# Neighbourhood attention in a fused two-block transformer: two PSUM banks each for scores and transposed probabilities, and the next item's transposition ahead of this item's values

## What is computed

```python
def neighbourhood_attention(q, k, v, rpb):
    ...
        sc = jnp.einsum('bchd,brcwhd->bhcrw', qr, kn) * scale + bias[None]
        sc = sc.reshape(bn, h, GRID_W, wh * ww).astype(jnp.float32)
        pr = jax.nn.softmax(sc, axis=-1).astype(v.dtype).reshape(bn, h, GRID_W, wh, ww)
        return jnp.einsum('bhcrw,brcwhd->bchd', pr, vn)
...
    h = h + (g_attn * y_attn + g_ssm * y_ssm) @ w_out[i]
```

## Time and profile before

| | |
|---|---|
| median of 3 runs | 3952.51 us (3952.14 to 3955.69) |
| the profiled execution | 3956.39 us |
| its span, first to last instruction | 3954.5 us |
| busy: PE, DVE, ACT, POOL | 91%, 61%, 28%, 51% of the span |
| mean granted TensorE clock | 0.951 of full speed |
| neighbourhood attention, `scores(0)` to the end of the last values | 3294.8 to 3433.8 us |
| its steady part, `scores(3)` on | from 3314.2 us |

### The profile page before, as it was taken

The page is one execution under the profiler, slowest core; times in us unless marked ns, Lnnn a source line. Parts: engine busy times, 40 slices in busy tenths (PEclk is TensorE's granted clock), DMA queues, the critical chain, the costliest instruction groups (busy, mean ns, idle before and its releaser), DMA issues.

```text
span 3954.5 us, 50521 instructions
## 1 busy us (share of the span) xinstructions
PE 3591.8 (91%) x20020; PEld 3070.1 (78%) x20020; DVE 2412.0 (61%) x3010; ACT 1094.4 (28%) x1848; POOL 2025.6 (51%) x1100
## 2 busy tenths in 40 slices
PE   8899788999999989788899999999957777999997
PEld 7798678899999779666778888888846664578886
DVE  7786798774333867688967333333278884563335
ACT  4406432222210422633132220121033334322201
POOL 4254235466666535433656666666633442356664
PEclk9799899999999979999999999999978888999999
DMA  3122111222223212111222223222311122222232
GB/s 133 44 89 73 33 44 64 64 87 89 90 91 101 97 48 86 59 38 43 80 69 93 93 96 101 96 95 96 106 55 59 62 77 88 73 87 94 95 109 72
DMA packets 91424, 313.29 MB, mean 79 GB/s; under 512 B 10240, under 2 KB 12544, under 8 KB 91264
## 3 DMA queue, kind: packets, MB, share of 16 engines
q1 hardware_dynamic: 80064, 289.44, 22.2%
q10 hardware_dynamic: 11200, 21.71, 1.5%
HBM read 304.82 MB, written 6.29 MB: 79 GB/s over the span
## 4 chain that ended last, share of the span: by engine, by line
PE 65%; DVE 23%; ACT 9%; issue 3%; POOL 0%; DMA 0%; ACTq 0%; DVEq 0%; POOLq 0%
PE acc L446 19%; PE acc L447 18%; PE acc L449 18%; DVE cu L1725 7%; DVE trs L1596 2%; PE aux L592 1%; DVE rh L1683 1%; PE aux L660 1%; PE aux L739 1%; DVE w L1884 1%; PE aux L675 1%; DVE zz L2006 1%; PE acc L689 1%; ACT yv L1349 1%; DVE rb L1680 1%
## 5 line engine op out<-in xcount | busy, mean ns | idle before, releaser
L419 POOL TENSOR_SCALAR whi<-raw 128x1024 fp32r<-128x1024 f32 x548 | 615.5, 1123 | 1855.0 <-PE acc L449 1834.0
L421 POOL TENSOR_TENSOR wlo<-raw,whi 128x1024 fp32r<-128x1024 f32 x548 | 1410.3, 2573 | 45.7
L446 PE MATMUL acc<-nhi,whi 128*128 128x512 f32 (+1 forms) x2776 | 956.7, 353 | 56.6 <-DVE mt L1734 25.7
L447 PE MATMUL acc<-nlo,whi 128*128 128x512 f32 (+1 forms) x2776 | 950.3, 351 | 0.0
L449 PE MATMUL acc<-nhi,wlo 128*128 128x512 f32 (+1 forms) x2776 | 871.3, 349 | 0.0
L446 PEld LDWEIGHTS acc<-nhi,whi 128*128 128x128 f32 x2776 | 528.7, 190 | 142.3 <-issue 53.4
L447 PEld LDWEIGHTS acc<-nlo,whi 128*128 128x128 f32 x2776 | 528.0, 190 | 68.3
L446 PE MATMUL acc<-bhi,whi 128*128 128x264 f32 (+1 forms) x1864 | 560.7, 317 | 17.9 <-ACT rg L1075 11.8
L447 PE MATMUL acc<-blo,whi 128*128 128x264 f32 (+1 forms) x1864 | 545.2, 309 | 0.0
L449 PEld LDWEIGHTS acc<-nhi,wlo 128*128 128x128 f32 x2776 | 489.2, 191 | 68.8
L1725 DVE SCALAR_TENSOR_TENSOR cu<-cx,par,cu 128x528 f32<-128x528 f32 (+1 forms) x480 | 489.6, 1074 | 0.0
(11 more groups left out here) (359 smaller groups left out, 4764.8 us busy)
## 6 DMA issues: line engine op xcount, KB each, us to landing
raw<-in_w SPq DMA_DIRECT2D x548, 512.0 KB, 3.3
merge_gates<-gout ACTq DMA_DIRECT2D x16, 256.0 KB, 2.8
natab<-in_natab ACTq DMA_DIRECT2D x4, 896.0 KB, 7.4
h<-in_h ACTq DMA_DIRECT2D x8, 264.0 KB, 6.6
rope<-in_rope ACTq DMA_DIRECT2D x2, 1056.0 KB, 7.1
rnn_w<-in_gate ACTq DMA_DIRECT2D x2, 1024.0 KB, 10.0
sbc<-in_ssm ACTq DMA_DIRECT2D x4, 512.0 KB, 3.5
sg<-merge_gates ACTq DMA_DIRECT2D x8, 256.0 KB, 3.5
```

The lines of the kernel that those rows point to most:

```text
L419: pool.tensor_scalar(hi, w, 1.0, 0.0, ALU.mult, ALU.add).then_inc(sem("w_hi"), 1)
L421: pool.tensor_tensor(lo, w, hi.bitcast(F32), ALU.subtract).then_inc(sem("w_split"), 1)
L446: pe.matmul(acc[s][:, f, 0:TH], hi, xh[:, f * TH:(f + 1) * TH], start=a, stop=False)
L447: pe.matmul(acc[s][:, f, 0:TH], hi, xl[:, f * TH:(f + 1) * TH], start=False, stop=False)
```

## The change

`scores(j)` writes bank `j % 2` of `aux[0]` and `turn(j)` bank `j % 2` of `aux[1]`; the readers on VectorE and ScalarE follow. `scores(j)` waits for the score step of item j - 2 and not j - 1, and `turn(j)` for the copy of j - 2 and not j - 1. `turn(j + 1)` stands between `merge_part(j)` and `values(j)`; it stood behind `values(j)`. The work itself, `pts2` and the lists of VectorE and ScalarE stay as they are.

```diff
@@ tensor engine, neighbours()
                 def scores(j):
...
-                    if j:
-                        pe.wait_ge(sem("na_scored"), j)
-                    pe.matmul(aux[0][:, 0, :], q2[rows, hh // 2, i * P:(i + 1) * P], k2[rows, hh // 2, :],
+                    if j >= 2:
+                        pe.wait_ge(sem("na_scored"), j - 1)
+                    pe.matmul(aux[0][:, j % 2, :], q2[rows, hh // 2, i * P:(i + 1) * P], k2[rows, hh // 2, :],
                               start=True, stop=True).then_inc(sem("na_s"), 1)
 
                 def turn(j):
                     pe.wait_ge(sem("na_p"), j + 1)
-                    if j:
-                        pe.wait_ge(sem("na_pt"), j)
+                    if j >= 2:
+                        pe.wait_ge(sem("na_pt"), j - 1)
                     for c in range(4):
-                        m = pe.transpose(aux[1][:, 0, c * P:(c + 1) * P], sm2[:, j % 3, c * P:(c + 1) * P], ident[:, :])
+                        m = pe.transpose(aux[1][:, j % 2, c * P:(c + 1) * P], sm2[:, j % 3, c * P:(c + 1) * P], ident[:, :])
...
                 scores(0)
                 scores(1)
+                turn(0)
                 for j in range(len(items)):
-                    turn(j)
                     if j + 2 < len(items):
                         scores(j + 2)
                     merge_part(j)
+                    if j + 1 < len(items):
+                        turn(j + 1)
                     values(j)
@@ scalar engine
-                    act.activation(pts2[:, :, :], aux[1][:, 0, :].rearrange("p (a b) -> p a b", a=4), ACT.Copy)\
+                    act.activation(pts2[:, :, :], aux[1][:, j % 2, :].rearrange("p (a b) -> p a b", a=4), ACT.Copy)\
@@ vector engine
-                    dve.tensor_tensor_reduce(sm2[:, b], aux[0][:, 0, :], add, 1.0, CHOSEN, ALU.add, ALU.max,
+                    dve.tensor_tensor_reduce(sm2[:, b], aux[0][:, j % 2, :], add, 1.0, CHOSEN, ALU.add, ALU.max,
```

## The result

| | before | changed |
|---|---|---|
| median of 4 runs | 3952.32 us (3950.69 to 3955.69) | 4003.82 us (3998.71 to 4009.52) |
| the profiled execution's span | 3954.5 us | 4007.6 us |
| granted clock, mean | 0.951 | 0.941 |

The ratio is 1.0128, with a 95% interval from 1.0113 to 1.0143: 51 us more. Forecast were 3992 us and a range up to 4004. The direction was right, and so was the loop between the two engines that makes the first half of the loss. The term for the low clock was less than half of what it measured, and the time is 12 us over the forecast. That it still lies in the range, by 0.2 us, is luck.

The account below looks back on a forecast made before the run. TensorE was taken to bound undisturbed items (3.55 us), VectorE's chain the borders of heads. Loop 26.2, start 1.1, end 0.8 and low clock 11 sum to +39.1 us: median about 3992 us, range 3977 to 4004.

Parts of the forecast that it names:

- The loop: Scores, VectorE's scaling, earlier transposition, values set the item period: 4.38 us undisturbed, 138.1 us for 28 periods, +26.2 us.
- Banks and copy: Second banks remove only the second scores product's wait; the copy into single pts2 stays hidden, 2.6 us to spare.
- Start and end: Stage's start up to scores(3) costs +1.1 us; its end, from scores(31) to the last values, +0.8 us.
- The neighbours: New instruction pairs on TensorE, values before scores and transposition before values: 0.1 us an item either way, taken as 0.
- The clock term: TensorE's new gaps in the stage bring some 26 us at the low clock level, costing 11 us.
- the clock falls and stays down longer: Rival for the stage: 45 us at the low level, all on the path, +50 us, 4003 us; chance 0.12.
- the clock holds: Rival: the stage's clock stays at 1.00 despite the longer gaps, +28 us, 3981 us; chance 0.22.
- What the profile was to show: In the stage: about 29 transposition waits for the scaling, 37 us; items of 4.4, 5.4 or 6.0 us; PEclk about 0.9.
- The rival of the faster side: Scaling is done before the earlier transposition, all the stage's waits go, 13.6 us gained, 3939 us; chance 0.04.

## Why the prediction came out as it did

**The loop was right, term by term.** Scores to transposition 2.69 us (2.70 forecast), undisturbed period 4.30 (4.38), with the product 5.36 (5.43), 28 periods at the full clock 136.4 (138.1, by the run with three unread matmuls), so +24.5 us where +26.2 was forecast. The 0.08 us is in the transposition, which the values follow 0.59 us behind its start and not 0.66: the 2.70 us ran from the scores' start in the timeline, which is 0.07 us ahead of their start in the chain, while 0.66 and 1.02 were lengths in the chain, so 0.07 us were counted twice.

**Banks and copy were right.** Nothing for the banks, and no matmul waits for the copy into the single `pts2`.

**Start and end were right.** From `scores(0)` (3295.47) to `scores(3)` 20.7 us where it was 19.4: +1.3, and +1.1 was forecast. The values of the last item end 3486.44 + 1.02 - 3478.88 = 8.6 us behind `scores(31)` (8.5 forecast).

**The neighbours were right in the bounds and wrong in the value.** In the changed kernel they are hidden by the wait, so 0 was right there. Out of the wait, they gain 0.15 us an item, a little more than the 0.1 allowed.

**The clock term failed.** Forecast were 26 us at the low level and 11 us of time, measured 78 us and 26.3 us. The step at fault is the scaling by the first block's attention: equal idle time was to bring equal low time, in stretches as short as the one of 3.3 us in the earlier trace rows. The price of a low microsecond, 11 / 26 = 0.42 forecast and 26.3 / 78 = 0.34 measured, was not at fault.

The number of falls was about right: in the trace of before the 27 us at 0.50 of the first block's attention are eight stretches of 3.4 us each, and here there are seven. Their length was not: four of the seven last 7 to 31 us, through items that follow one another with no gap (the row from 3361.2 to 3376.5 above). So a gap could cost whole items of 6.60 us, not one stretch.

The rival "the clock falls and stays down longer", which had 0.12, is what happened; it was priced at 4003 us from 45 us at the low level, all on the path, where there are 78, partly on it. That 4003 is so near the measured 4003.82 is therefore luck as well, and the range reached to 4004 only because half of this rival was taken in.

The Trainium skill (TensorE: Matmul & The Clock Gate, a second failure mode) tells of a kernel that cycles through PSUM banks, idles briefly and often between groups of matmuls, and has its clock swing by it. The trace agrees on the short idling, with 0.76, though not on the banks: the kernel with the banks alone lost nothing, and the order alone, with one bank each, had 0.72.

**One reading for the rival "the clock holds" was wrong.** It says that the stage stood at 1.00 through waits up to 1.6 us. That wait, 1.57 us ahead of 3307.06, is at the start, where the clock was low: the transposition behind it took 1.12 us. In the part at 1.00 no wait for the scaling was over 0.8 us, so that rival had less for it than its 0.22.

**What the profile was to show.** Forecast were 29 waits and 37 us for the scaling and a clock of about 0.9; the stage behind its start has 24 waits, 31 us and 0.76. The waits are fewer because in the items without a gap, all at 0.50, the scaling is done before TensorE gets to the transposition.

**The rival of the faster side** named the right point of decision, when the scaling ends, and took VectorE's list as a given. It was that list that could move: there the waits do go. The 3939.56 us are near the 3939 of that rival, but not by its sum: the gain was 15.6 us where it had 13.6, and 4.2 of it are the neighbours, which it had at nothing.

**Left open.** Why the low level outlasts its gap at some borders of this stage, with TensorE busy all the time, and not at others or in the first block's attention, was not settled. Filling the gaps shows that they bring it on, not what ends it.

## What to carry to other kernels

When an instruction is moved ahead on one engine, look up what stands in front of its input in the other engine's list. An engine that is early only waits, and all that was moved behind the wait joins the loop; here the cure was to move the producer too, and that alone had most of the gain. And where a change opens gaps on TensorE, price the low clock as a cost of its own, with a wide range: here it was as dear as the loop itself, and a few unread matmuls took it away.

## What the runs showed of the hardware

- At 0.50 an item without a gap takes 6.60 us where 4.30 with a gap is the rule at 1.00, and the clock stayed at 0.50 through 15.3 us in which TensorE was busy all the time.
- In the order branch product, transposition, values the first weight load of a transposition starts at 3318.64 with the last matmul of the product, 0.23 us ahead of the first transposition at 3318.87; four transpositions then take 0.44 us of the chain. Behind the values, in the kernel before, load and transposition start together, and four take 0.59:

```profile
3317.13 0.42 PEld L747 LDWEIGHTS aux<-ident,sm 128*128 128x128 f32 x4 [0.17 <-issue]
```

The Trainium skill (TensorE: Matmul & The Clock Gate, Part 2, first step) says that weight loads can be pulled ahead of matmuls in flight, when their row groups do not conflict or the load goes to a background buffer; the rows agree that it happens behind one kind of matmul and not behind the other, and do not show which condition decides.
- 93 matmuls of 512 columns more made a kernel 23 us faster (4003.82 to 3980.5 us); its clock in the stage went from 0.76 to 1.00.
